# A diffusion backbone on one core: modulation sums through four 32-column groups, feed-forward loops of TensorE written out, two operands moved to 64 bytes

## The chip, the cores and the metric

The kernel runs on one core of one Trainium2 chip, in fp32. The metric is the device time of one execution in microseconds (us). TensorE (PE) multiplies, VectorE (DVE), ScalarE (ACT) and GpSimd (POOL) do elementwise work, SyncE (SP) and POOL issue transfers. PEld are TensorE's weight loads.

## The reference, cut to what matters

Two layers work on 256 latent and 256 context tokens of 1024 channels. Each has a feed-forward (2816 hidden), a mixer and a second feed-forward, and every one of them is scaled and shifted by modulation vectors, which come from one vector-matrix product with a weight of 1024 x 9216 per layer.

```python
def _swiglu(x, w_gu, w_down):
    g, u = jnp.split(x @ w_gu, 2, axis=-1)
    return (jax.nn.silu(g) * u) @ w_down
...
    silu_c = jax.nn.silu(c)
    silu_cc = jax.nn.silu(c_ctx)[None]
    h, hc = x, ctx
    for l in range(DEPTH):
...
        mod = (silu_c @ w_mod[l] + b_mod[l]).reshape(B, N_MOD, D_MODEL)
        mod_c = (silu_cc @ w_mod[l] + b_mod[l]).reshape(1, N_MOD, D_MODEL)
        m = [mod[:, i] for i in range(N_MOD)]
...
        h = h + 0.5 * m[2][:, None] * _swiglu(_modulate(_rms(h, norm_w[l, 0]), m[0], m[1]),
                                              ffn1_w_gu[l], ffn1_w_down[l])
...
        u = _modulate(_rms(h, norm_w[l, 1]), m[3], m[4])
        y, yc = _hybrid_mixer(u, uc, ctx_out, w_in[l], w_out[l], ...)
        h = h + m[5][:, None] * y
        h = h + 0.5 * m[8][:, None] * _swiglu(_modulate(_rms(h, norm_w[l, 2]), m[6], m[7]),
                                              ffn2_w_gu[l], ffn2_w_down[l])
```

## The kernel before, in words

Channels lie on partitions, the 512 tokens (latent and context) on the free axis. All weights of the feed-forwards and the mixer come as one stream of 320 blocks of 128x1024 (512 KB), loaded by SP into four places of `raw`. Every matmul is done as three, for precision: ACT rounds a block into `whi`, DVE subtracts to get `wlo` (L603), both with two places, and TensorE multiplies hi by hi, hi by lo and lo by hi (`three`, L997 to L999). A block is 24 matmuls.

A feed-forward has 44 gate and up blocks (moving operand `xh`, `xl`) and 22 down blocks (moving operand `ah`, `al`, the hidden values split in two), the latter in two halves of 11 with four banks of `ps` each. Three feed-forwards (f = 0, 1, 2) work on 512 columns, the last on 256. TensorE, ACT and DVE run the gate and up blocks in loops of four blocks, the down blocks in loops of four with the rest written out.

The modulation is cut into 36 units of 512 output columns. Units 0 to 3 are done at the start on TensorE itself (`mod_start`: a stationary operand of 2 columns, L1033, four units in four groups of 32 output partitions). For the other 32 units, POOL loads four pairs of weight rows a unit (`wm`, two places), DVE multiplies and accumulates them into `macc` (a part of `shared_a`; `mod_pair`, L621 and L625), which leaves 128 partial sums for each column and stream. `mod_sums` (L1049) then adds these over partitions: for each of four column chunks and two streams a matmul with the 128x128 products as stationary operand and a column of ones as the moving one, into a bank of `ps`; `mod_columns` on DVE (L635) adds the bias into `modc`. The sum of a unit is issued in the middle of the second block of the next round of four, and DVE may not start the next unit before it has added those columns. Units 4 to 14 belong to f = 0, unit 15 to the first mixer, 16 to 26 to f = 1, 27 to 35 to f = 2. `gate_columns` and `norm` need complete columns.

The order on each engine is the order in the code. An fp32 matmul stands as two records in the trace, an fp32r one (all of `three`) as one. In memory, `ah` and `al` start 32 bytes past a multiple of 64, since `qws` in front of them has 8 bytes and is padded to 32; `xh`, `xl`, `whi`, `wlo` start at multiples of 64.

## Time and profile before

| what | us |
|---|---|
| median of 3 runs (lowest, highest) | 1797.49 (1795.21, 1800.09) |
| span of the profiled execution | 1794.2 |
| PE busy | 1725.9 (96%) |
| PE weight loads busy | 1448.0 (81%) |
| DVE busy | 1087.9 (61%) |
| ACT busy | 613.4 (34%) |

The profiled execution has no separate time of its own; its span is 3.3 us below the median of the runs, the part that lies outside the first and last instruction. PE's busy time includes the depth of the array, so neighbouring matmuls overlap in it: what a matmul costs is read from start to start.

### The profile page before, as it was taken

Reading aid. Unit: us, or ns where it says so; the run is one execution under the profiler, and the core shown is the slowest. Engines: PE = TensorE matmul, PEld = TensorE weight load, DVE = VectorE, ACT = ScalarE, POOL = GpSimd, SP = SyncE. Lnnn points to the kernel's source line nnn. Section 1 sums busy time; section 2 is a strip of 40 time slices with the busy share of each in tenths; the row PEclk is TensorE's granted clock in tenths of the full one; section 3 lists DMA queues with packets and bytes.
Section 4 is the critical chain, followed back from the end, with each engine's and each line's share of the span. In section 5 each row is a group of like instructions: output and inputs, shape, how many; then the busy total and the mean of one; then the engine's idle time right before and its main releaser. Section 6 shows DMA issues by size and latency. Waiting matters only on the chain.

```text
span 1794.2 us, 25623 instructions
## 1 busy us (share of the span) xinstructions
PE 1725.9 (96%) x8952; PEld 1448.0 (81%) x8952; DVE 1087.9 (61%) x1668; ACT 613.4 (34%) x909; POOL 79.3 (4%) x144
## 2 busy tenths in 40 slices
PE   3999999999998999999999999999999999889999
PEld 1888888887786778888888878888888878589999
DVE  2877777235678667777761377777523277665554
ACT  3322222124534543222221242222222264554443
POOL 0000000000001000000000000000000000000000
PEclk9999999999999999999999999999999999999999
DMA  9455555322241125555552225555332224135554
GB/s 360 136 180 177 181 180 177 96 91 71 94 129 47 36 71 176 182 172 183 174 165 94 94 83 187 177 180 181 107 97 96 86 83 142 35 123 182 185 178 153
DMA packets 69685, 248.64 MB, mean 139 GB/s; under 512 B 7424, under 2 KB 8448, under 8 KB 69504
## 3 DMA queue, kind: packets, MB, share of 16 engines
q1 hardware_dynamic: 51200, 180.79, 30.9%
q0 software_dynamic: 18432, 67.12, 11.5%
q8 instruction: 36, 0.59, 0.1%
q14 instruction: 17, 0.14, 0.0%
HBM read 246.83 MB, written 1.05 MB: 138 GB/s over the span
## 4 chain that ended last, share of the span: by engine, by line
PE 89%; DVE 6%; ACT 2%; issue 1%; SPq 1%; DMA 1%; DVEq 0%; ACTq 0%
PE ps L997 28%; PE ps L999 28%; PE ps L998 27%; PE ps L1049 3%; DVE shared_b L704 1%; DVE xl L690 1%; PE ps L1188 1%; DMA raw<-wstream 1%; DVE wlo L603 1%; DVE nmax L895 1%; PE ps L1215 1%; ACT prob L505 1%; SPq L274 1%; ACT whi L343 0%; PE ps L1136 0%
## 5 line engine op out<-in xcount | busy, mean ns | idle before, releaser
L603 DVE TENSOR_TENSOR wlo<-raw,whi 128x1024 fp32r<-128x1024 f32 x320 | 392.2, 1226 | 607.6 <-ACT whi L343 606.8
L997 PE MATMUL ps<-xh,whi 128*128 128x512 f32 (+1 forms) x1880 | 679.8, 362 | 23.6 <-DVE xl L690 19.2
L343 ACT ACTIVATE whi<-raw 128x1024 fp32r<-128x1024 f32 x320 | 339.1, 1060 | 1061.9 <-PE ps L999 1045.2
L999 PE MATMUL ps<-xh,wlo 128*128 128x512 f32 (+1 forms) x1880 | 663.2, 353 | 0.0
L998 PE MATMUL ps<-xl,whi 128*128 128x512 f32 (+1 forms) x1880 | 662.5, 352 | 0.0
L997 PEld LDWEIGHTS ps<-xh,whi 128*128 128x128 f32 x1880 | 358.9, 191 | 82.3 <-issue 25.3
L998 PEld LDWEIGHTS ps<-xl,whi 128*128 128x128 f32 x1880 | 360.3, 192 | 49.3 <-issue 3.8
L999 PEld LDWEIGHTS ps<-xh,wlo 128*128 128x128 f32 x1880 | 359.8, 191 | 47.2
L625 DVE SCALAR_TENSOR_TENSOR shared_a<-wm,cs,shared_a 128x512 f32<-128x512 f32 x448 | 307.5, 746 | 0.0
L997 PE MATMUL ps<-ah,whi 128*128 (+2 forms) x704 | 258.6, 367 | 0.3 <-DVE wlo L603 0.3
L998 PE MATMUL ps<-al,whi 128*128 (+2 forms) x704 | 258.3, 367 | 0.0
L999 PE MATMUL ps<-ah,wlo 128*128 (+2 forms) x704 | 258.2, 367 | 0.0
L997 PEld LDWEIGHTS ps<-ah,whi 128*128 128x128 f32 x704 | 132.3, 188 | 24.5 <-issue 0.5
L999 PEld LDWEIGHTS ps<-ah,wlo 128*128 128x128 f32 x704 | 132.4, 188 | 24.1
L998 PEld LDWEIGHTS ps<-al,whi 128*128 128x128 f32 x704 | 132.4, 188 | 23.8
L304 POOL DMA_DIRECT2D wm<-wmod x126 | 66.6, 528 | 1143.7 <-DVEq L628 1136.0
L1049 PEld LDWEIGHTS ps<-K,shared_a 128*128 128x128 f32 x512 | 62.1, 192 | 2.7
L1049 PE MATMUL ps<-K,shared_a 128*128 128x1 f32 x512 | 58.9, 245 | 0.0
L649 DVE TENSOR_TENSOR al<-shared_b,ah 128x512 f32 (+3 forms) x88 | 54.4, 618 | 1.8 <-ACT ah L363 1.2
L642 DVE TENSOR_TENSOR shared_b<-shared_b,ps 128x512 f32<-128x512 f32 (+1 forms) x88 | 54.1, 614 | 0.6 <-ACT shared_b L358 0.5
L363 ACT ACTIVATE ah<-shared_b 128x512 f32 (+3 forms) x88 | 49.4, 561 | 5.6 <-DVE shared_b L642 5.6
L440 ACT ACTIVATE xh<-shared_b,modc 128x256 fp32r<-128x256 f32 x88 | 43.5, 508 | 22.6 <-DVE shared_b L704 22.6
(106 smaller groups left out, 872.7 us busy)
## 6 DMA issues: line engine op xcount, KB each, us to landing
raw<-wstream SPq DMA_DIRECT2D x320, 512.0 KB, 3.4
wm<-wmod POOLq DMA_DIRECT2D x128, 512.0 KB, 3.6
wm<-wmod SPq DMA_DIRECT2D x3, 2048.0 KB, 21.1
h<-x_t SPq DMA_DIRECT2D x1, 2048.0 KB, 12.0
wm<-wmod SPq DMA_DIRECT2D x2, 1024.0 KB, 20.4
K<-cols SPq DMA_DIRECT2D x1, 1163.0 KB, 14.3
out_t<-h SPq DMA_DIRECT2D x8, 128.0 KB, 2.5
K<-cols SPq DMA_DIRECT2D x1, 269.0 KB, 2.9
```

The source lines that it names most:

```text
L304: pool.dma_start(wm[:, c, :, :].rearrange("p a n -> p (a n)"), wmod[bass.ds(i * 2 + c, 1)].rearrange("a p n -> p (a n)"))\
L343: act.activation(whi[:, n % SPL, :, :].rearrange("p a b -> p (a b)"), raw[:, s, :], ACT.Copy)\
L363: act.activation(ah[:, bass.ds(i * (2 * T) + j * T, w)], af[:, j % 2, 0:w], ACT.Copy)\
L440: act.activation(xh[:, d, s * S:(s + 1) * S], xt[:, (g - 1) % 4, :], ACT.Identity, bias=modc[:, N_MOD * l + 3 * st, d, s:s + 1]).then_inc( ...
L603: dve.tensor_tensor(wlo[:, n % SPL, :, :].rearrange("p a b -> p (a b)"), raw[:, n % RAW, :], whi[:, n % SPL, :, :].rearrange("p a b -> p ( ...
L625: ins = dve.scalar_tensor_tensor(acc, src, sc, acc, ALU.mult, ALU.add)
L642: dve.tensor_tensor(af[:, j % 2, 0:w], sil[:, j % 2, 0:w], ps[:, 2 * (j % 2) + 1, 0:w], ALU.mult)\
L649: dve.tensor_tensor(al[:, dst], af[:, j % 2, 0:w], ah[:, dst].bitcast(F32), ALU.subtract)\
L997: pe.matmul(out_ap, hi_w, hi_x, start=start, stop=False)
L998: pe.matmul(out_ap, hi_w, lo_x, start=False, stop=False)
L999: return pe.matmul(out_ap, lo_w, hi_x, start=False, stop=stop)
L1049: ins = pe.matmul(ps[:, bank, 2 * c + v:2 * c + v + 1], macc[:, v, c * P:(c + 1) * P], col("one", 0, 1), start=True, stop=True)
```

## The change

`mod_sums` takes a selector as the stationary operand: 32 columns of `pick`, all zero but one, which stands at row r = 2 x unit (counted within the feed-forward) + stream. The products are the moving operand, 128 columns at a time, one chunk for each of four groups of 32 output partitions. Row r of each group gets the sums of that unit and stream; the others get zero added. So the sums of all units of a feed-forward gather in one bank. Once per feed-forward, DVE copies the bank into `mrows` (`mod_rows_out`), TensorE turns it (`mod_turn`), and DVE adds all biases at once (`mod_columns`), all in the first down half. There the banks of the two halves are chosen anew (`DN_BANKS`). Unit 15 moves from the first mixer into the first down half of f = 0, and the sum of the last unit of a full set from the end of that half to its second block. DVE waits for the sum of the unit before instead of adding its columns. TensorE's loops over blocks are written out, so are DVE's down loops. `qws` gets 64 bytes and `mrows` 512, so `shared_a`, `shared_b`, `ah`, `al` and what shares their place now start at multiples of 64 bytes.

```diff
-MIX_UNIT = 15
+LATE_UNIT = 15
+SET_ENDS = {0: 16, 1: 27, 2: 36}
-                  ("ident", P), ("poolw", DEPTH * 2 * P)):
+                  ("ident", P), ("poolw", DEPTH * 2 * P), ("pick", 64)):
...
-        qws = sb("qws", [P, DEPTH])
+        qws = sb("qws", [P, 16])
+        mrows = sb("mrows", [P, P])
...
@@ -611,6 +617,9 @@
             def mod_pair(u, p, i=0):
 
                 base = unit_steps(u)
+                if p == 0:
+
...
 
-            def mod_columns(u, n=1, i=0, bank=5):
-
-                dve.wait_ge(mod_sum, i + (u + n))
-                a = COLS["b_mod"][0] + u * UC
-                flat = modc[:, :, :, :].rearrange("p a b c -> p (a b c)")
-                dve.tensor_tensor(flat[:, bass.ds(i * UC + u * UC, n * UC)], ps[:, bank, 0:n * UC],
-                                  K[:, bass.ds(i * UC + a, n * UC)], ALU.add).then_inc(mod_col, n)
+            def mod_rows_out(f):
+
+                dve.wait_ge(mod_sum, SET_ENDS[f])
+                dve.tensor_copy(mrows[:, :], ps[:, ROWS_BANK, 0:P]).then_inc(mod_rows, 1)
+
+            def mod_columns(f):
+
+                u0, n = UNIT_AT[f][0], SET_ENDS[f] - UNIT_AT[f][0]
+                dve.wait_ge(mod_turned, f + 1)
+                turned = ps[:, TURN_BANK, 0:P].rearrange("p (j u v) -> p u j v", j=HN // P, v=2)[:, 0:n, :, :]
+                bias = col("b_mod", u0 * UC, n * UC).rearrange("p (u j v) -> p u j v", u=n, v=2)
+                flat = modc[:, :, :, :].rearrange("p a b c -> p (a b c)")[:, u0 * UC:(u0 + n) * UC]
+                dve.tensor_tensor(flat.rearrange("p (u j v) -> p u j v", u=n, v=2), turned, bias, ALU.add)\
+                    .then_inc(mod_col, n)
 
             def hidden(f, j, i, w):
...
@@ -724,23 +740,17 @@
                         elif e or not first:
 
                             hidden_low(f, e // 2 - 1, i, w)
-                        if e == 0 and columns:
-                            mod_columns(u0 - 1, 1, i)
                         if unit:
                             mod_pair(u0, e, i)
 
-                body(0, nu > 0, False, True)
+                body(0, nu > 0, True)
                 if nu:
                     with dve.Fori(1, nu) as i:
-                        body(i, True, True)
-                if 0 < nu < GU // 4:
-                    with dve.Fori(nu, nu + 1) as i:
-                        body(i, False, True)
-                if nu + 1 < GU // 4:
-                    with dve.Fori(nu + 1, GU // 4) as i:
-                        body(i, False, False)
+                        body(i, True)
+                if nu < GU // 4:
+                    with dve.Fori(max(nu, 1), GU // 4) as i:
+                        body(i, False)
                 hidden_low(f, -1, GU // 4, w)
-                gate_columns(m)
 
                 def half_out(hf, ds):
                     for d in ds:
...
@@ -756,12 +766,16 @@
 
                 for hf in range(2):
                     nd = n0 + GU + HALF * hf
-                    split_next(nd)
-                    with dve.Fori(0, (HALF - 3) // 4) as i:
-                        for e in range(4):
-                            split_next(nd + 1 + e, i, 1)
-                    if hf == 0 and nu == GU // 4:
-                        mod_columns(u0 + nu - 1, bank=0)
+                    for b in range(HALF - 2):
+                        split_next(nd + b)
+                        if hf == 0 and f == 0 and 1 <= b <= PAIRS:
+                            mod_pair(LATE_UNIT, b - 1)
+                        if hf == 0 and nu and b == HALF - 4:
+                            mod_rows_out(f)
+                    if hf == 0:
+                        if nu:
+                            mod_columns(f)
+                        gate_columns(m)
 
                     for b in (HALF - 2, HALF - 1):
                         if hf == 0:
...
@@ -860,10 +874,6 @@
                         lambda_ends()
                     if 1 <= b <= QKB:
                         rope(l, b - 1)
-                    if l == 0 and QKB < b <= QKB + PAIRS:
-                        mod_pair(MIX_UNIT, b - QKB - 1)
-                    if l == 0 and b == QKB + PAIRS + 2:
-                        mod_columns(MIX_UNIT)
                     if b in (CV - 3, CV - 2):
 
                         dve.wait_ge(evac, EV[l] + b)
...
-            def mod_sums(u, i=0, bank=5):
-
-                pe.wait_ge(mod_acc, i * (2 * DC) + unit_steps(u + 1))
-
-                pe.wait_ge(mod_col, i + u)
-                for c in range(HN // P):
-                    for v in range(2):
-                        ins = pe.matmul(ps[:, bank, 2 * c + v:2 * c + v + 1], macc[:, v, c * P:(c + 1) * P],
-                                        col("one", 0, 1), start=True, stop=True)
+            def mod_sums(f, u):
+
+                pe.wait_ge(mod_acc, unit_steps(u + 1))
+                for v in range(2):
+                    r = 2 * (u - UNIT_AT[f][0]) + v
+                    for j in range(HN // P):
+                        ins = pe.matmul(ps[32 * j:32 * j + 32, ROWS_BANK, 0:P], col("pick", 31 - r, 32),
+                                        macc[:, v, j * P:(j + 1) * P], start=r == 0,
+                                        stop=u + 1 == SET_ENDS[f] and v == 1)
                 ins.then_inc(mod_sum, 1)
+
+            def mod_turn(f):
+
+                pe.wait_ge(mod_rows, f + 1)
+                pe.transpose(ps[:, TURN_BANK, 0:P], mrows[:, :], col("ident", 0, P)).then_inc(mod_turned, 1)
 
             def norm_stat(m):
...
-                    for e in range(2 if first else 0, 4):
-                        if e % 2 == 0 and not first:
-
-                            pe.wait_ge(mul_done, i * 2 + (F0 + e // 2 - 1))
-
-                        column_block(n0 + e, e, w, i, 1,
-                                     between=(lambda: mod_sums(u0 - 1, i)) if e == 1 and sums else None)
-
-                body(0, False, True)
+                first_blocks(m, n0)
+                for i in range(GU // 4):
+                    for e in range(2 if i == 0 else 0, 4):
+                        if e % 2 == 0 and i:
+
+                            pe.wait_ge(mul_done, F0 + 2 * i + e // 2 - 1)
+                        sums = e == 1 and 1 <= i <= nu
+                        column_block(n0 + 4 * i + e, e, w,
+                                     between=(lambda u=u0 + i - 1: mod_sums(f, u)) if sums else None)
+
+                def down(hf, b):
+                    n = n0 + GU + HALF * hf + b
+                    pe.wait_ge(lo_done, n + 1)
+                    if hf == 0:
+
+                        pe.wait_ge(al_done, F0 + 2 * b + 2)
+
+                    last = b == HALF - 1 and hf == 1
+                    for r, d in [(r, d) for d in range(4) for r in range(2)] if last else \
+                            [(r, d) for r in range(2) for d in range(4)]:
+                        if hf == 0 and b == 0 and d == 3:
+
+                            pe.wait_ge(mul_done, F0 + FC - 1)
+                        src = slice((2 * b + r) * T, (2 * b + r) * T + w)
+                        ins = three(ps[:, DN_BANKS[hf][d], 0:w], whi[:, n % SPL, 4 * r + d, :],
+                                    wlo[:, n % SPL, 4 * r + d, :], ah[:, src], al[:, src],
+                                    b == 0 and r == 0, b == HALF - 1 and r == 1)
+                        if last and r == 1 and d < 3:
+                            ins.then_inc(dn_done, 1)
+                    ins.then_inc(block_done, 1)
+
+                for b in range(HALF):
+                    down(0, b)
+                    if nu == GU // 4 and b == 1:
+                        mod_sums(f, u0 + nu - 1)
+                    if f == 0 and b == 6:
+                        mod_sums(f, LATE_UNIT)
+                    if nu and b == 8:
+                        mod_turn(f)
                 if nu:
-                    with pe.Fori(1, min(nu + 1, GU // 4)) as i:
-                        body(i, True)
-                if nu + 1 < GU // 4:
-                    with pe.Fori(nu + 1, GU // 4) as i:
-                        body(i, False)
-                for hf in range(2):
-                    nd = n0 + GU + HALF * hf
-                    b0 = 4 if hf == 0 else 0
-
-                    def down(b, i=0, k=0):
-                        n = nd + b
-                        pe.wait_ge(lo_done, i * (4 * k) + (n + 1))
-                        if hf == 0:
-
-                            pe.wait_ge(al_done, i * (8 * k) + (F0 + 2 * b + 2))
-
-                        last = b == HALF - 1 and hf == 1
-                        for r, d in [(r, d) for d in range(4) for r in range(2)] if last else \
-                                [(r, d) for r in range(2) for d in range(4)]:
-                            src = bass.ds(i * (8 * T * k) + (2 * b + r) * T, w)
-                            ins = three(ps[:, b0 + d, 0:w], whi[:, n % SPL, 4 * r + d, :],
-                                        wlo[:, n % SPL, 4 * r + d, :], ah[:, src], al[:, src],
-                                        b == 0 and r == 0, b == HALF - 1 and r == 1)
-                            if last and r == 1 and d < 3:
-                                ins.then_inc(dn_done, 1)
-                        ins.then_inc(block_done, 1)
-
-                    if nu:
-
-                        pe.wait_ge(mod_col, u0 + (min(nu, GU // 4 - 1) if hf == 0 else nu))
-                    down(0)
-                    with pe.Fori(0, (HALF - 3) // 4) as i:
-                        for e in range(4):
-                            down(1 + e, i, 1)
-                    if hf == 0 and nu == GU // 4:
-
-                        mod_sums(u0 + nu - 1, bank=0)
-                    down(HALF - 2)
-                    down(HALF - 1)
+
+                    pe.wait_ge(mod_col, SET_ENDS[f])
+                    pe.wait_ge(mod_rows, f + 1)
+                for b in range(HALF):
+                    down(1, b)
...
@@ -1148,12 +1156,8 @@
                         column_block(n0 + b, b % 4, T if b < 4 else w)
                     if 1 <= b <= QKB:
                         stat(b - 1)
-                    if l == 0 and b == QKB + PAIRS + 1:
-                        mod_sums(MIX_UNIT)
 
                 pe.wait_ge(rq_done, 8 * (l + 1))
-                if l == 0:
-                    pe.wait_ge(mod_col, MIX_UNIT + 1)
                 for b in range(VB):
                     n = n0 + CV + b
                     pe.wait_ge(lo_done, n + 1)
```

TensorE, gate and up of f = 0, second block of a round, where a unit's sum stands between two chunks (`K` holds the constants, `shared_a` the products). Before:

```order
L998 MATMUL ps<-xl,whi 128x512
L999 MATMUL ps<-xh,wlo 128x512
L1044 REGISTER_ALU
L1046 REGISTER_ALU
L1049 MATMUL ps<-K,shared_a 128x1 x8
L997 MATMUL ps<-xh,whi 128x512
L998 MATMUL ps<-xl,whi 128x512
```

After:

```order
L1008 MATMUL ps<-xl,whi 128x512
L1009 MATMUL ps<-xh,wlo 128x512
L1058 MATMUL ps<-shared_a,K 32x128 x8
L1007 MATMUL ps<-xh,whi 128x512
L1008 MATMUL ps<-xl,whi 128x512
```

The eight matmuls stay where they were; their output is 32x128 instead of 128x1, and the register arithmetic of the loop is gone.

DVE, f = 0, from the end of the gate and up loop to the end of the first down half (`wlo` is the split of a weight block, `mrows` the copied bank). Before:

```order
L649 TENSOR_TENSOR al<-shared_b,ah 128x512
L655 TENSOR_SCALAR gcol<-modc 128x16
L603 TENSOR_TENSOR wlo<-raw,whi 128x1024
L760 UNCONDITIONAL_BRANCH
...
L603 TENSOR_TENSOR wlo<-raw,whi 128x1024
L760 REGISTER_ALU
L760 COMPARE_AND_BRANCH
L635 TENSOR_TENSOR modc<-ps,K 128x8
L603 TENSOR_TENSOR wlo<-raw,whi 128x1024 x2
L661 SCALAR_TENSOR_TENSOR h<-ps,gcol,h 128x256 x4
```

After:

```order
L609 TENSOR_TENSOR wlo<-raw,whi 128x1024 x2
L630 TENSOR_SCALAR shared_a<-wm,cs 128x512 x2
L634 SCALAR_TENSOR_TENSOR shared_a<-wm,cs,shared_a 128x512 x2
L609 TENSOR_TENSOR wlo<-raw,whi 128x1024
L634 SCALAR_TENSOR_TENSOR shared_a<-wm,cs,shared_a 128x512 x4
...
L609 TENSOR_TENSOR wlo<-raw,whi 128x1024 x3
L642 COPY mrows<-ps 128x128
L609 TENSOR_TENSOR wlo<-raw,whi 128x1024
L651 TENSOR_TENSOR modc<-ps,K 128x96
L671 TENSOR_SCALAR gcol<-modc 128x16
L609 TENSOR_TENSOR wlo<-raw,whi 128x1024 x2
```

The passes of unit 15 stand between the splits, and the copy, the add of all columns and the gate columns near the end of the half.

## Rows read from the trace of the kernel before

**Rows 1.** The page: busy time and share, granted clock, chain by line.
```profile
PE 1725.9 (96%) x8952; PEld 1448.0 (81%) x8952; DVE 1087.9 (61%) x1668; ACT 613.4 (34%) x909; POOL 79.3 (4%) x144
PEclk9999999999999999999999999999999999999999
PE ps L997 28%; PE ps L999 28%; PE ps L998 27%; PE ps L1049 3%; DVE shared_b L704 1%; DVE xl L690 1%; PE ps L1188 1%; DMA raw<-wstream 1%; DVE wlo L603 1%; DVE nmax L895 1%; PE ps L1215 1%; ACT prob L505 1%; SPq L274 1%; ACT whi L343 0%; PE ps L1136 0%
```

**Rows 2.** Chain that ended last, in time: start, length, engine, output, line, records.
```profile
75.15 1.68 PE ps L1049 x16
98.75 1.68 PE ps L1049 x16
```

**Rows 3.** Timeline of PE around one sum: start, length, engine, line, operation, output<-inputs, form.
```profile
74.75 0.40 PE L999 MATMUL ps<-xh,wlo 128*128 128x512 f32 x1
74.98 1.84 PE L1049 MATMUL ps<-K,shared_a 128*128 128x1 f32 x16
76.69 0.48 PE L997 MATMUL ps<-xh,whi 128*128 128x512 f32 x1
...
79.54 0.39 PE L997 MATMUL ps<-xh,whi 128*128 128x512 f32 x1
...
98.35 0.40 PE L999 MATMUL ps<-xh,wlo 128*128 128x512 f32 x1
```

**Rows 4.** Timeline of PE at the start, units 0 to 3 (three windows).
```profile
22.80 0.59 PE L1060 MATMUL ps<-shared_a,K 128*128 128x512 f32 x1
...
23.33 0.61 PE L1033 MATMUL ps<-wm,cs 128*2 128x512 f32 x4
...
23.33 3.62 PE L1033 MATMUL ps<-wm,cs 128*2 128x512 f32 x32
```

**Rows 5.** Groups by line and form: count, busy us, mean ns, idle before.
```profile
L625 DVE SCALAR_TENSOR_TENSOR shared_a<-wm,cs,shared_a 128x512 f32<-128x512 f32 x448 | 307.5, 746 | 0.0
...
L1215 PE MATMUL ps<-difT,vt 128*128 128x128 f32 x160 | 23.0, 283 | 8.7 <-ACT difT L515 8.7
...
L1033 PE MATMUL ps<-wm,cs 128*2 128x512 f32 x64 | 7.6, 592 | 4.3 <-DMA wm<-wmod 4.3
```

**Rows 6.** Timeline of PE in the mixer's attention.
```profile
579.54 1.16 PE L1215 MATMUL ps<-difT,vt 128*128 128x128 f32 x8 [0.88 <-ACT difT L515]
```

**Rows 7.** Timeline of PE: down, value blocks, gate and up, down with 256 columns.
```profile
304.18 0.40 PE L997 MATMUL ps<-ah,whi 128*128 128x512 f32 x1
...
354.34 0.40 PE L999 MATMUL ps<-ah,wlo 128*128 x1
...
539.68 0.39 PE L997 MATMUL ps<-whi,xh 128*128 128x512 f32 x1
...
545.58 0.39 PE L999 MATMUL ps<-whi,xl 128*128 128x512 f32 x1
...
1639.78 0.28 PE L998 MATMUL ps<-xl,whi 128*128 128x256 f32 x1
...
1643.26 0.28 PE L997 MATMUL ps<-xh,whi 128*128 128x256 f32 x1
...
1786.69 0.28 PE L999 MATMUL ps<-ah,wlo 128*128 128x256 f32 x1
...
1791.31 0.28 PE L999 MATMUL ps<-ah,wlo 128*128 128x256 f32 x1
```

**Rows 8.** Timeline of DVE: gate and up, then down; in brackets idle time and releaser.
```profile
100.69 0.17 DVE L635 TENSOR_TENSOR modc<-ps,K 128x8 f32 x1 [0.35 <-PE ps L1049]
...
111.23 1.23 DVE L603 TENSOR_TENSOR wlo<-raw,whi 128x1024 fp32r<-128x1024 f32 x1 [0.96 <-ACT whi L343]
...
322.27 1.23 DVE L603 TENSOR_TENSOR wlo<-raw,whi 128x1024 fp32r<-128x1024 f32 x1 [4.37 <-ACT whi L343]
```

**Rows 9.** Timeline of PE where the first mixer's scores begin.
```profile
558.49 1.02 PE L1188 MATMUL ps<-kq 128*128 128x512 f32 x2
```

More of the change, by code:

```diff
@@ L66 @@
 UNIT_AT = {0: (4, GU // 4), 1: (16, GU // 4), 2: (27, 9)}
-MIX_UNIT = 15
+LATE_UNIT = 15
+SET_ENDS = {0: 16, 1: 27, 2: 36}
+ROWS_BANK, TURN_BANK = 5, 1
+DN_BANKS = ((4, 6, 7, 0), (1, 2, 3, 5))
 COLS = {}
@@ L72 @@
 for _name, _n in (("c", DC * 2), ("norm_w", DEPTH * 3 * DC * 2), ("b_mod", DEPTH * N_MOD * DC * 2),
-                  ("eps", 1), ("one", 1), ("sel", 8), ("ones", P),
+                  ("eps", 1), ("sel", 8), ("ones", P),
                   ("qw", DEPTH), ("kw", DEPTH), ("subln", DEPTH), ("conv", DEPTH * 2 * 3),
@@ L176, in program @@
         mod_sum = sem("mod_sum")
+        mod_rows = sem("mod_rows")
+        mod_turned = sem("mod_turned")
         mod_col = sem("mod_col")
@@ L613, in mod_pair @@
                 base = unit_steps(u)
+                if p == 0:
+                    dve.wait_ge(mod_sum, i + u)
                 dve.wait_ge(wm_in[p % 2], i * (16 * PAIRS // 2) + 16 * (((u - START_UNITS) * PAIRS + p) // 2 + 1))
@@ L717, in ffn, with body @@
                 u0, nu = UNIT_AT.get(f, (0, 0))
-                def body(i, unit, columns, first=False):
+                def body(i, unit, first=False):
                     for e in range(4):
@@ L840, in lambda_sums @@
                 dve.sem_inc(lam_red, 1)
-                own(dve.tensor_scalar(qws[:, :], col("qw", 0, DEPTH), DH ** -0.5, None, ALU.mult))
+                own(dve.tensor_scalar(qws[:, 0:DEPTH], col("qw", 0, DEPTH), DH ** -0.5, None, ALU.mult))
             def lambda_ends():
@@ L999, in three, with column_block @@
                 return pe.matmul(out_ap, lo_w, hi_x, start=False, stop=stop)
-            def column_block(n, bank, w, i=0, k=0, ready=None, a=0, last=True, between=None):
-                pe.wait_ge(lo_done, i * (4 * k) + (n + 1))
+            def column_block(n, bank, w, ready=None, a=0, last=True, between=None):
+                pe.wait_ge(lo_done, n + 1)
                 for c in range(DC):
@@ L1069, in ffn @@
                 F0 = FC * f
-                def body(i, sums, first=False):
-                    if first:
-                        first_blocks(m, n0)
-                    for e in range(2 if first else 0, 4):
-                        if e % 2 == 0 and not first:
-                            pe.wait_ge(mul_done, i * 2 + (F0 + e // 2 - 1))
-                        column_block(n0 + e, e, w, i, 1,
-                                     between=(lambda: mod_sums(u0 - 1, i)) if e == 1 and sums else None)
@@ L1347 @@
         "eps": np.full((P, 1), EPS),
-        "one": np.ones((P, 1)),
+        "pick": np.repeat((np.arange(64) == 31)[None], P, 0),
         "sel": np.stack([np.arange(P) == 32 * u + v for u in range(4) for v in range(2)], 1),
```

6 lines of the change are left out of this document (3 added, 3 removed).

## The prediction

> **What bounds the kernel now.** I read the page from the top: PE is busy 96% of the span and DVE 61%, and the clock digits are 9 in all forty slices, so the array is at its upper level (2.4 GHz) nearly throughout [rows 1]. The chain that ended last runs through PE for almost all of its length, and one small line in it has 3%: L1049, the modulation sums. The bound is therefore the pitch of TensorE (start of one matmul to start of the next) and the number of matmuls, not a wait. Next I read the chain in order of time: the 32 sums stand in it one by one (two are shown), each 16 records in 1.68 us [rows 2], that is 0.105 us a record although only one column is moved: with one moving column the time is that of loading 128 columns of products as the stationary operand. 32 x 1.68 = 53.8 us, the 3%.
>
> **What one sum really costs.** In the timeline of TensorE around one sum [rows 3] the last matmul before it starts at 74.75, the sum at 74.98, the next matmul at 76.69. From 79.54 to 98.35 there are 83 pitches, 18.81/83 = 0.2266 us, and the back edge of the written loop lies among them: it costs nothing. From 76.69 to 79.54 there are 12 pitches in 2.85 us where 2.72 were due: 0.13 us are lost after the sum. So a sum costs 1.71 + 0.13 = 1.84 us, and the chain's period agrees: 98.75 - 75.15 = 23.60 [rows 2], and 96 x 0.2266 + 1.84 = 23.59. Of 32 sums that is 58.9 us, 3.3% of the span; this is the pot that the first edit draws on.
>
> **Part 1, sums by four column groups.** Removed are, for each unit, 8 matmuls with the products stationary (16 records, since fp32 runs as two). Added are 8 matmuls with a 128x32 selector stationary and 128 columns of products moving, again 16 records, written to four different groups of 32 partitions. What four groups do side by side is in this trace: the start of the program has the same scheme with 2-column stationaries. Four records stand there within 0.61 us although each takes 0.592, and 32 records took 3.62 us, so (3.62 - 0.61)/7 = 0.43 us a burst of four [rows 4, 5]. A burst of four costs what one record of 512 columns costs. Scaled to 128 columns that is 0.107 us; the nearest row with 128 moving columns in fp32 is L1215, 8 records in 1.16 us of which the last is 0.28 long, so (1.16 - 0.28)/7 = 0.126 us [rows 5, 6]. I take 0.126, because its stationary loads are of real size: four bursts are 0.50 us.
> Going into the groups: the last 128-wide record before the start's grouped ones began at 22.80, the first grouped one at 23.33 [rows 4]; 0.53 where 0.43 was due, so 0.10 us. Coming out: no row shows it. Its low bound is zero, its high one the whole length of a 128-column record less its pitch, 0.28 - 0.11 = 0.17; I take 0.17 because the other direction wasn't free. The 0.13 after the sum stays. Sum: 0.10 + 0.50 + 0.17 + 0.13 = 0.90 us instead of 1.84, a gain of 0.94, and 32 x 0.94 = 30.1 us. Low bound for a sum: 4 x 0.107 = 0.43 with nothing around it, a gain of 45 us. High bound with groups that still overlap: 1.3 us (another 0.11 for the first loads of 32 columns, and bursts of 0.2), a gain of 17 us.
> The row shows 0.10 us on the way into the groups. The Trainium skill (TensorEngine Tiling (Array Packing), Key Properties) says that changing the tiling mode, and not merely the tile, drains the engine; the trace agrees in kind. The rule speaks against this edit, because it is paid twice in each of 32 places; by a full drain both ways (0.17 each instead of 0.10 and 0.17) the sum would be 0.97 us and the gain 28 us.
>
> **Part 2, ah and al moved from 32 to 64 bytes.** `qws` grows from 2 to 16 columns, and everything allocated behind it, from `shared_a` on, starts at a multiple of 64 bytes; before it was 32 past one. The down matmuls (moving ah, al) have a pitch of (354.34 - 304.18)/215 = 0.2333 us, those of gate and up (moving xh, xl, which lie on 64 already) 0.2266 [rows 3, 7]. The difference is 6.7 ns, 16 cycles at 2.4 GHz. It isn't the change of bank after every third matmul: the value blocks of the mixer change it just so and run at (545.58 - 539.68)/26 = 0.2269 [rows 7]. It isn't the loop either, since it begins with the first block, which is written out. Three feed-forwards of 512 columns have 22 x 24 = 528 such matmuls each: 1584 x 6.7 ns = 10.6 us. The last feed-forward has 256 columns, and there the picture is turned round: ah at (1791.31 - 1786.69)/39 = 0.1185, xh at (1643.26 - 1639.78)/29 = 0.1200 [rows 7]. So alignment gives nothing there and could cost 528 x 1.5 ns = 0.8 us; I take zero, with that as bound. Since the 256-column rows don't show the effect, the 10.6 us are the less certain part.
>
> **Part 3, loops of TensorE written out.** Nothing: the back edges cost nothing above, and the straight-line value blocks run at the same pitch as the looped ones.
>
> **Part 4, the turn.** Each of three feed-forwards gets a copy of 128x128 and one add of 96 columns on DVE, and one 128-column transpose on TensorE: 0.126 + 0.13 behind it, about 0.25 us, 0.8 us for three. In exchange 32 small adds on DVE go. The copy is queued behind the split of block 7 of the down part, some 3 us before TensorE reaches the end of block 8, where the turn stands; DVE idles 4.37 us of every 5.6 there (24 x 0.2333) [rows 8]. TensorE's new wait for the columns stands ahead of the second half, two blocks later. Both are covered; uncovered, each would cost the DVE chain of about 1 us, 3 us in all. The selector adds 63 columns to a load of constants, most of them in its second, late part, and the bank numbers change no instruction; both nothing.
>
> **Part 5, unit 15 from mixer to down part.** Its four pairs (16 DVE passes of 0.746 us, 2.98 a block [rows 5]) go into the idle 4.37 us of blocks 1 to 4, its four loads with them. They leave the mixer, where TensorE starts the first scores at 558.49 with no idle time noted ahead of them [rows 9], so nothing is won there beyond the sum already counted. On DVE the first pair of every unit now waits for the sum before it, at the place where the column add waited before (0.35 us [rows 8]); the sum is shorter, so this gets less. In the gate and up loop the period falls from 23.6 to 22.7 us, all of it in the block that holds the sum; in the fullest blocks, of 5.44 us, DVE still waits 0.96 us for ACT, which waits for TensorE [rows 8]: DVE does not take over. If it did, the bound is the 0.96 us of that block against the 0.94 that the period falls, so nothing comes on top of the forecast's range.
>
> **The sum.** 1794.2 - 30.1 - 10.6 + 0.8 = 1754.3 us of span. The median of the runs, 1797.49, lies 3.3 above the profiled span, so I expect **1757.6 us**, 2.2% less.
>
> **Rivals.**
> (a) The groups overlap, but alignment isn't the cause of the 6.7 ns. For it speaks that the 256-column rows go the other way, and that after a sum even the aligned xh runs at (79.54 - 76.69)/12 = 0.2375 for a while [rows 3]. Time: 1768.
> (b) The groups work in bursts that don't overlap with each other: each of four bursts takes a record's full length and its loads, 0.28 + 0.11, so 1.56 + 0.40 = 1.96 us a sum, no gain; only alignment is left: 1797.5 - 10.6 + 0.8 + 3.8 = 1791. Against it: the bursts at the start follow at 0.43 with records of 0.59.
> (c) The other side, **slower**: the 32-column loads and the moving columns take turns in the array, so that 16 records go one by one, at 0.105 for the load and 0.107 for the columns: 3.4 us + 0.4 = 3.8 us a sum, 32 x 1.96 = 63 us more, less 9.8: 1850. It decides the sign from 2.15 us a sum on (1.84 + 9.8/32). For it: no row has a 32-column stationary in this mode, and both records of one product go to the same group. Against it: the start has the same two records to a group, and overlaps four.
> (d) A sum near its low bound, 0.5 to 0.6 us: 1797.5 - 41 - 10 = 1746.
>
> **How the numbers follow.** Forecast (sum of 0.7 to 1.2 us, alignment works) 0.62; (a) 0.16; (d) 0.10; (b) 0.07; (c) 0.04; 0.01 for another loss. The forecast's own bounds are 1751 (0.7 us) and 1767 (1.2 us). The range has to reach into (a) and (d): 1747 to 1771 leaves out about 2 in 10. This kernel's measurement can tell about 0.3% from no change: (b) lies on that border and is split. Faster by over 0.3%: 0.92; within: 0.04; slower: 0.04.
>
> **What would show it.** In the profile of the changed kernel: the 16 records of a sum at 0.4 to 0.6 us from first to last start; 22.66 us from one sum to the next instead of 23.60; pitch of the down matmuls 0.2267 instead of 0.2333, and 0.1185 to 0.1200 in the last feed-forward; no idle time of TensorE ahead of the turns and of the second down halves. It would be wrong if the sum's records start 0.1 us apart one by one, if the down pitch stays at 0.2333, or if DVE's split becomes the releaser of gate and up matmuls.

## The result, and the profile after

The changed kernel takes 1756.43 us (median; 1754.53 to 1756.91), the kernel before beside it 1798.53 us: a ratio of 0.9763, 95% interval 0.975 to 0.9776. It is 42.1 us faster; 1757.6 had been forecast. The profiled span fell from 1794.2 to 1755.1 us, by 39.1; why that is less stands under "The sum of it" below.

The page of the changed kernel: busy time, granted clock, chain by line (`three` is now L1007 to L1009, the sums L1058).

```profile
PE 1687.6 (96%) x8955; PEld 1405.1 (80%) x8955; DVE 1082.3 (62%) x1642; ACT 613.9 (35%) x909; POOL 79.3 (5%) x144
...
PEclk9999999999999999999999999999999999999999
...
PE ps L1007 29%; PE ps L1008 28%; PE ps L1009 28%; PE ps L1058 1%; DVE shared_b L720 1%; PE ps L1192 1%; DMA raw<-wstream 1%; DVE wlo L609 1%; DVE nmax L905 1%; PE ps L1219 1%; DVE xl L706 1%; SPq L280 1%; ACT prob L511 1%; PE ps L1144 0%; ACT whi L349 0%
```

TensorE is still the bound. The sums have gone from 3% of the chain [rows 1] to 1%. The chain in order of time, as [rows 2]:

```profile
74.81 0.57 PE ps L1058 x16
97.41 0.57 PE ps L1058 x16
```

Sixteen records and the way back now take 0.57 us instead of 1.68, and the period is 22.60 instead of 23.60 us. The timeline of TensorE around a sum, as [rows 3]:

```profile
74.42 0.39 PE L1009 MATMUL ps<-xh,wlo 128*128 128x512 f32 x1
74.74 0.64 PE L1058 MATMUL ps<-shared_a,K 128*32 128x128 f32 x16
75.31 0.50 PE L1007 MATMUL ps<-xh,whi 128*128 128x512 f32 x1
...
78.66 0.39 PE L1009 MATMUL ps<-xh,wlo 128*128 128x512 f32 x1
```

In: 74.74 - 74.42 - 0.2267 = 0.09 us. The sixteen records and the way out: 0.57. Behind it: 14 pitches in 3.35 us where 3.17 were due, 0.18. Together 0.84 us a sum. The last of the sixteen records starts 0.37 us behind the first (0.64 less its own length of 0.27), so they overlap.

The down part, 48 matmuls of 512 columns, then 256 columns (before in [rows 7]), and the turn between them in time:

```profile
293.75 0.39 PE L1007 MATMUL ps<-ah,whi 128*128 128x512 f32 x1
...
304.40 0.39 PE L1009 MATMUL ps<-ah,wlo 128*128 128x512 f32 x1
...
344.16 0.39 PE L1009 MATMUL ps<-ah,wlo 128*128 128x512 f32 x1
344.39 0.27 PE L1066 MATMUL ps<-K,mrows 128*128 128x128 f32 x1
344.42 0.48 PE L1007 MATMUL ps<-ah,whi 128*128 128x512 f32 x1
...
349.29 0.39 PE L1007 MATMUL ps<-ah,whi 128*128 128x512 f32 x1
...
1699.73 0.28 PE L1007 MATMUL ps<-ah,whi 128*128 128x256 f32 x1
...
1710.88 0.28 PE L1007 MATMUL ps<-ah,whi 128*128 128x256 f32 x1
```

(304.40 - 293.75)/47 = 0.2266 us, where it was 0.2333; with 256 columns (1710.88 - 1699.73)/93 = 0.1199, where it was 0.1185. The turn has no idle time ahead of it. DVE in the first down half, where it now works on unit 15 (idle time before a split in brackets, as [rows 8]):

```profile
318.78 2.73 DVE L634 SCALAR_TENSOR_TENSOR shared_a<-wm,cs,shared_a 128x512 f32<-128x512 f32 x4
323.08 1.23 DVE L609 TENSOR_TENSOR wlo<-raw,whi 128x1024 fp32r<-128x1024 f32 x1 [1.56 <-ACT whi L349]
...
341.38 0.28 DVE L642 COPY mrows<-ps 128x128 f32<-128x128 f32 x1
```

Of the idle 4.37 us of a block 1.56 are left: the passes fit, and the copy is done 2.7 us before the turn.

### The profile page after: what moved, and what is told of

The parts are those of the page before. It is cut to its first block, busy times and chain, and to the rows that moved or that the text cites. A ratio compares the mean times of both kernels' runs of the same rounds, so it can differ in the third digit from the quotient of the medians.

```text
span 1755.1 us, 24815 instructions
## 1 busy us (share of the span) xinstructions
PE 1687.6 (96%) x8955; PEld 1405.1 (80%) x8955; DVE 1082.3 (62%) x1642; ACT 613.9 (35%) x909; POOL 79.3 (5%) x144
## 4 chain that ended last, share of the span: by engine, by line
PE 90%; DVE 6%; ACT 2%; SPq 1%; issue 1%; DMA 1%; DVEq 0%; ACTq 0%
PE ps L1007 29%; PE ps L1008 28%; PE ps L1009 28%; PE ps L1058 1%; DVE shared_b L720 1%; PE ps L1192 1%; DMA raw<-wstream 1%; DVE wlo L609 1%; DVE nmax L905 1%; PE ps L1219 1%; DVE xl L706 1%; SPq L280 1%; ACT prob L511 1%; PE ps L1144 0%; ACT whi L349 0%
## 5 line engine op out<-in xcount | busy, mean ns | idle before, releaser
L1007 PE MATMUL ps<-xh,whi 128*128 128x512 f32 (+1 forms) x1880 | 682.4, 363 | 23.4 <-DVE xl L706 18.3
L1009 PE MATMUL ps<-xh,wlo 128*128 128x512 f32 (+1 forms) x1880 | 664.4, 353 | 0.0
L1007 PEld LDWEIGHTS ps<-xh,whi 128*128 128x128 f32 x1880 | 359.5, 191 | 87.6 <-issue 31.0
L1009 PEld LDWEIGHTS ps<-xh,wlo 128*128 128x128 f32 x1880 | 360.6, 192 | 47.6
L1007 PE MATMUL ps<-ah,whi 128*128 128x512 f32 (+1 forms) x704 | 255.9, 364 | 0.0
L1008 PE MATMUL ps<-al,whi 128*128 128x512 f32 (+1 forms) x704 | 255.4, 363 | 0.0
L1009 PE MATMUL ps<-ah,wlo 128*128 128x512 f32 (+1 forms) x704 | 255.3, 363 | 0.0
L1007 PEld LDWEIGHTS ps<-ah,whi 128*128 128x128 f32 x704 | 132.3, 188 | 21.3 <-issue 0.6
L1009 PEld LDWEIGHTS ps<-ah,wlo 128*128 128x128 f32 x704 | 132.3, 188 | 20.6
L677 DVE SCALAR_TENSOR_TENSOR h<-ps,gcol,h 128x256 f32<-128x256 f32 x88 | 38.2, 478 | 18.6 <-PE ps L1009 18.6
L364 ACT ACTIVATE shared_b<-ps 128x512 f32<-128x512 f32 (+1 forms) x88 | 46.5, 528 | 0.0
## 6 DMA issues: line engine op xcount, KB each, us to landing
h<-x_t SPq DMA_DIRECT2D x1, 2048.0 KB, 11.7
```

The lines of the kernel that those rows point to most:

```text
L364: act.activation(sil[:, j % 2, 0:w], ps[:, 2 * (j % 2), 0:w], ACT.Silu).then_inc(silu_done, 1)
L1007: pe.matmul(out_ap, hi_w, hi_x, start=start, stop=False)
L1008: pe.matmul(out_ap, hi_w, lo_x, start=False, stop=False)
L1009: return pe.matmul(out_ap, lo_w, hi_x, start=False, stop=stop)
```

## The experiments

Every time below is a median; each kernel has its own ratio to the kernel before, run beside it. Its medians in these runs lie between 1798.53 and 1800.22 us, so a difference of two medians from different runs is good to some 2 us; the pitches and periods of the traces are finer. A "visit" is one stay of TensorE in the four groups.

### Alignment: the edit alone, and undone

The kernel before with the wider `qws` alone:

```diff
-        qws = sb("qws", [P, DEPTH])
+        qws = sb("qws", [P, 16])
...
```

> The kernel before with one edit: qws has 16 columns, so that ah and al (and all behind qws) start on 64 bytes. Theory (alignment of the moving operand sets the pitch of the 512-column down matmuls): pitch 0.2333 becomes 0.2267 in three feed-forwards, 1584 x 6.7 ns = 10.6 us less, and 528 x 1.6 ns = 0.8 us more in the last feed-forward, where the pitch goes from 0.1184 to 0.1200; together 9.8 us less, about 1788 us. Rival (the pitch comes from the order of banks or from the place of the down part in the program): 0.2333 stays, no change.

Measured: 1790.52 us, ratio 0.994 (0.9917 to 0.9963), 9.5 us under the 1800.03 of the kernel before beside it. The down pitch is (350.93 - 309.90)/181 = 0.2267:

```profile
309.90 0.39 PE L999 MATMUL ps<-ah,wlo 128*128 128x512 f32 x1
...
350.93 0.39 PE L997 MATMUL ps<-ah,whi 128*128 x1
```

The changed kernel with ah and al alone moved back by 32 bytes:

```diff
         hidden = ExitStack()
+        hidden.enter_context(nc.sbuf_tensor("hpad", [P, 8], F32))
```

> The changed kernel with 32 bytes of padding in front of ah, so that ah and al alone start at 32 past a multiple of 64; all else as changed. Theory (it is the moving operand of the down matmuls that counts): the pitch returns to 0.2333 with 512 columns and to 0.1184 with 256, 9.8 us more than the changed kernel, about 1766 us. Rival (it is another of the operands that moved with them, for example what DVE and ACT write at the same time): the pitch stays at 0.2267 and the time at 1756 us.

Measured: 1765.29 us, ratio 0.9806 (0.9784 to 0.9828), 8.9 us over the changed kernel. 512 columns, then 256:

```profile
294.75 0.40 PE L1008 MATMUL ps<-ah,whi 128*128 128x512 f32 x1
...
300.82 0.40 PE L1010 MATMUL ps<-ah,wlo 128*128 128x512 f32 x1
...
1719.75 0.28 PE L1009 MATMUL ps<-al,whi 128*128 128x256 f32 x1
...
1730.50 0.28 PE L1008 MATMUL ps<-ah,whi 128*128 128x256 f32 x1
```

26 pitches of 0.2335, and 92 of 0.1168. So it is the place of ah and al and no other operand. With 256 columns the pitch is even shorter than before the change (0.1185), although both start "32 past 64". The addresses of the built programs tell the two apart: before, ah and al start 96 past a multiple of 128, here 32 past one.

### The same for xh and xl

```diff
+        xpad0 = sb("xpad0", [P, 8])
         xh = sb("xh", [P, DC, T], F32R)
         xl = sb("xl", [P, DC, T], F32R)
+        xpad1 = sb("xpad1", [P, 8])
```

> The changed kernel with 32 bytes of padding in front of xh and again behind xl, so that xh and xl start at 32 past a multiple of 64 and all else stays on 64. Theory: every 512-column matmul with xh or xl moving goes from 0.2267 to 0.2333: 3 x 44 x 24 = 3168 in gate and up, and about 20 x 24 = 480 in the first mixer, 3648 x 6.7 ns = 24 us more; those with 256 columns go from 0.1200 to 0.1184, 1056 + some 500, 2.5 us less; about 1778 us. Rival (a property of ah and al or of the down part): 1756 us.

Measured: 1774.8 us, ratio 0.9862 (0.9836 to 0.9888), 18.4 us over the changed kernel. Gate and up with 512 columns, down with 512, gate and up with 256, down with 256:

```profile
59.72 0.39 PE L1011 MATMUL ps<-xh,wlo 128*128 128x512 f32 x1
...
70.46 0.39 PE L1009 MATMUL ps<-xh,whi 128*128 128x512 f32 x1
...
369.67 0.39 PE L1009 MATMUL ps<-ah,whi 128*128 128x512 f32 x1
...
380.43 0.39 PE L1011 MATMUL ps<-ah,wlo 128*128 128x512 f32 x1
...
1619.78 0.28 PE L1010 MATMUL ps<-xl,whi 128*128 128x256 f32 x1
...
1630.28 0.28 PE L1010 MATMUL ps<-xl,whi 128*128 128x256 f32 x1
...
1726.94 0.28 PE L1009 MATMUL ps<-ah,whi 128*128 128x256 f32 x1
...
1739.90 0.28 PE L1011 MATMUL ps<-ah,wlo 128*128 128x256 f32 x1
```

Gate and up: 46 pitches of 0.2335, as the theory says. The two paddings together also moved ah and al by 64 bytes, to 64 past a multiple of 128, which I hadn't meant to matter; their pitch is (380.43 - 369.67)/47 = 0.2289, between 0.2267 and 0.2333. With 256 columns xh runs at 90 pitches of 0.1167, and ah at (1739.90 - 1726.94)/110 = 0.1178. So the 256-column matmuls with xh gained twice what I had put down for them, but ah and al lost 1584 x 2.2 ns = 3.5 us that the forecast didn't have, and gained 528 x 2.2 ns = 1.2 us. With the forecast's counts the pitches give 24.8 - 5.1 + 3.5 - 1.2 = 22 us, close to the forecast's 21.5, and not the 18.4 of the medians; the difference isn't explained, and the interval of this run alone is 5 us to each side.

### Loops of TensorE written out, in the kernel before

```diff
-                    with pe.Fori(1, min(nu + 1, GU // 4)) as i:
-                        body(i, True)
...
+                for i in range(1, GU // 4):
+                    body(i, 1 <= i <= nu)
...
-                    with pe.Fori(0, (HALF - 3) // 4) as i:
+                    for i in range((HALF - 3) // 4):
```

> The kernel before with TensorE's loops over blocks written out and nothing else. Theory: back edges cost nothing on a TensorE that is never waiting for its sequencer, so no change: 1797.5 us within 1. Rival (the loops cost where the trace doesn't show it, or straight-line code starves TensorE, since it must be fetched, 0.6 MB more of it): a change of 2 us or more either way.

Measured: 1797.52 us, ratio 0.999 (0.9979 to 1.0001). The interval holds 1, but it also holds a gain of 2 us or more, so the times alone don't rule out the rival. The chain does, for the back edges and for starving in gate and up: one period is 23.60 us, to the hundredth that of the looped kernel [rows 2].

```profile
74.06 1.68 PE ps L1049 x16
97.66 1.68 PE ps L1049 x16
```

DVE's written-out down loops weren't run by themselves.

### Sums: how the 0.84 us is made up

Every unit's grouped matmuls issued twice:

```diff
+                for v in range(2):
+                    r = 2 * (u - UNIT_AT[f][0]) + v
+                    for j in range(HN // P):
+                        ins = pe.matmul(ps[32 * j:32 * j + 32, spare, 0:P], col("pick", 31 - r, 32),
+                                        macc[:, v, j * P:(j + 1) * P], start=True, stop=True)
                 ins.then_inc(mod_sum, 1)
...
```

> The changed kernel with every unit's eight grouped matmuls issued a second time, straight behind the first and into another bank that nobody reads. It measures the second sixteen records without a second change of shape around them. Theory (the sum of 0.85 us is some 0.43 to 0.50 us of four bursts and the rest is going in and out of the groups and the slow pitch after it): 32 x 0.43 to 0.50 = 14 to 16 us more. Rival (bursts are all of it, nothing is fixed): 0.85 each, 27 us more.

Measured: 1768.16 us, ratio 0.9827 (0.9811 to 0.9844), 11.7 us over the changed kernel, where 14 to 16 were expected. In the chain the period is 23.00 us, 0.40 more than 22.60:

```profile
73.93 0.57 PE ps L1058 x16
96.93 0.57 PE ps L1058 x16
```

Sixteen further records cost 0.40 us of the period, so of a sum's 0.84 the other 0.44 are paid once a visit. The timeline gives the parts:

```profile
73.86 0.64 PE L1058 MATMUL ps<-shared_a,K 128*32 128x128 f32 x16
...
74.88 0.50 PE L1007 MATMUL ps<-xh,whi 128*128 128x512 f32 x1
...
78.18 0.39 PE L1009 MATMUL ps<-xh,wlo 128*128 128x512 f32 x1
```

From the first record to the next 128-wide start it is 1.02 us, 0.57 in the changed kernel: sixteen records take 0.44 to 0.45, 0.11 a burst of four, and the way out is 0.57 - 0.44 = 0.13. Behind the visit 14 pitches take 3.30 us, 0.13 too many and not 0.18; that is the step from 0.44 to the 0.40 of the period, and why the slow stretch is shorter here stays open. The records cost what was expected of them (0.43 to 0.50); that the stretch behind them gets shorter was not foreseen.

The sums of all units but the first of each set left out:

```diff
                 pe.wait_ge(mod_acc, unit_steps(u + 1))
+                if u > UNIT_AT[f][0]:
+                    pe.sem_inc(mod_sum, 1)
+                    return
...
```

> The changed kernel with the grouped matmuls of the first unit of each set alone; those of the other 29 units are left out (their modulation is missing from the output), the signals stay. Theory: 29 x 0.85 = 24.7 us less than the changed kernel, about 1732 us, if TensorE stays the bound to the end. Rival (DVE's accumulation of the next unit or the weight splits become the bound once the sum is gone): a smaller gain, with idle time of TensorE ahead of gate and up blocks.

Measured: 1731.05 us, ratio 0.9617 (0.9601 to 0.9633), 25.4 us less than the changed kernel (24.7 expected), 0.88 us a sum. The waits of TensorE for the split (microseconds in total, times, longest) stay as small as in the changed kernel, where they are 3.0 us:

```profile
PE ps L1007 <- DVE wlo L609: 3.7, 4, 1.5
```

So neither DVE nor ACT takes over when the sums are gone.

### Is it the groups or the smaller stationary operand

All eight matmuls sent to one group:

```diff
-                        ins = pe.matmul(ps[32 * j:32 * j + 32, ROWS_BANK, 0:P], col("pick", 31 - r, 32),
+                        ins = pe.matmul(ps[0:32, ROWS_BANK, 0:P], col("pick", 31 - r, 32),
...
```

> The changed kernel with the eight 32-column matmuls of a unit all sent to the same group of 32 output partitions (the four chunks are added together, so the modulation is wrong). Theory (the gain comes from four groups at once): the sixteen records follow each other at 0.107 to 0.126 us, a sum costs 1.7 to 2.0 us plus some 0.4 around it, 2.1 to 2.4 us, 40 to 50 us more than the changed kernel, as slow as before or slower. Rival (the gain comes from small stationary loads, not from groups at once): 1756 to 1765 us.

Measured: 1796.13 us, ratio 0.9981 (0.9972 to 0.9991), 39.7 us over the changed kernel.

Selectors of 128 columns, across the whole array:

```diff
-                        ins = pe.matmul(ps[32 * j:32 * j + 32, ROWS_BANK, 0:P], col("pick", 31 - r, 32),
+                        ins = pe.matmul(ps[:, ROWS_BANK, 0:P], col("pick", 127 - 32 * j - r, P),
...
```

> The changed kernel with selectors of 128 columns instead of 32: the same eight matmuls with products moving and the same result in the bank, but across the whole array, with no change of shape and nothing side by side. Theory: sixteen records at 0.126 us and 0.13 behind, 2.15 us a sum, 32 x 1.3 = 42 us more than the changed kernel, about 1798 us. Rival (loads of 128 columns hide behind the moving columns): 0.107 a record, 1.85 us, 32 us more.

Measured: 1788.53 us, ratio 0.9937 (0.9921 to 0.9954), 32.1 us over the changed kernel. The chains, first of one group, then of the wide selector:

```profile
74.53 1.86 PE ps L1058 x16
98.38 1.86 PE ps L1058 x16
```

```profile
75.10 1.78 PE ps L1058 x16
98.68 1.78 PE ps L1058 x16
```

The way into the wide selector's records:

```profile
74.70 0.40 PE L1009 MATMUL ps<-xh,wlo 128*128 128x512 f32 x1
74.94 1.95 PE L1058 MATMUL ps<-shared_a,K 128*128 128x128 f32 x16
```

Periods of 23.85 and 23.58 us against 21.76 without a sum (96 x 0.2267): 2.09 and 1.82 us a sum. The rival of the second run was right: loads of 128 columns hide behind 128 moving columns, at some 0.11 us a record (1.78/16), so turning the operands round gains nothing and costs nothing by itself (1.82 against 1.84). The whole gain of the first edit is the four groups at once; with one group the fixed part of the visit makes it dearer than before. The wide selector, which changes no shape of the stationary operand, pays 0.01 us on the way in (74.94 - 74.70 - 0.2267), where four groups and one pay 0.09: so that part goes with the change to 32 columns. The wide kernel lies 11.2 us under the 1799.74 of the kernel before beside it; alignment explains 9.8 of them by the pitches, 32 x 0.02 us the sums, and the rest is within the spread.

### The last feed-forward started 32 bytes further on, and the changed kernel once more

```diff
+OFF = (0, 0, 0, 8)
+XOFF = (0, 0, 0, 0, 0, 8)
...
-                        src = slice((2 * b + r) * T, (2 * b + r) * T + w)
+                        src = slice((2 * b + r) * T + OFF[f], (2 * b + r) * T + OFF[f] + w)
...
-                            xh[:, c, a:w], xl[:, c, a:w], c == 0, c == DC - 1)
+                            xh[:, c, a + off:w + off], xl[:, c, a + off:w + off], c == 0, c == DC - 1)
```

> The changed kernel, and in the last feed-forward (256 columns) xh, xl, ah and al are written and read 8 columns (32 bytes) further on in their places, so that the moving operands of 1056 gate and up and 528 down matmuls start 32 past a multiple of 64. All else as changed. Theory (with 256 columns the 32-byte start is the quicker one, as ah before the change): pitch 0.1200 becomes 0.1184 in both, 1584 x 1.6 ns = 2.5 us less than the changed kernel, about 1754 us. Rival (0.1184 belongs to the down part alone): only 0.8 us less, and gate and up stay at 0.1200.

Measured: 1753.16 us, ratio 0.9735 (0.9721 to 0.9748). Gate and up run at (1622.90 - 1620.43)/21 = 0.1176, down at (1710.39 - 1699.78)/91 = 0.1166.

```profile
1620.43 0.28 PE L1011 MATMUL ps<-xh,wlo 128*128 128x256 f32 x1
...
1622.90 0.28 PE L1011 MATMUL ps<-xh,wlo 128*128 128x256 f32 x1
...
1699.78 0.28 PE L1010 MATMUL ps<-al,whi 128*128 128x256 f32 x1
...
1710.39 0.28 PE L1011 MATMUL ps<-ah,wlo 128*128 128x256 f32 x1
```

> The changed kernel once more, as it is, on the chip of the run before it. It gives the time to compare that run with, and a second profile: the three stretches at half clock that were 6.8 us long in the first profile where the kernel before had 3.4 may be shorter again (theory: how long TensorE stays at the lower clock after a pause varies from run to run, worth 1 to 3 us of span) or the same (rival: the changed order of work fixes them).

Measured: 1755.85 us, ratio 0.9758 (0.9745 to 0.9772). The run before it is 2.7 us faster than this one; the intervals of the two touch, so it is the pitches that show the effect, and the time only agrees. By the pitches the gain should be 1056 x 2.4 ns + 528 x 3.3 ns = 4.3 us; the same edit on top of the pairs below gave 4.6.

The clock of two stretches of 9 us, each with a restart of TensorE after a norm: the first feed-forward of the second layer, and the last feed-forward (columns as given by the profile: stretch, length, busy time of PE, PEld, DVE, ACT, POOL, granted clock, DMA share, GB/s). The kernel before, the changed kernel, and the changed kernel once more:

```profile
659.00:668.00 9.00, 6.75 (x35) 5.91 (x36) 8.96 (x24) 6.44 (x14) 0.00 (x0) 0.81 0.17 61
1598.00:1607.00 9.00, 7.73 (x46) 7.18 (x47) 7.11 (x16) 4.89 (x9) 0.00 (x0) 0.81 0.19 60
```

```profile
645.00:654.00 9.00, 7.90 (x34) 7.12 (x34) 9.00 (x24) 5.93 (x13) 0.00 (x0) 0.62 0.19 58
1557.00:1566.00 9.00, 7.09 (x32) 6.79 (x33) 6.48 (x17) 4.69 (x9) 0.00 (x0) 0.62 0.19 58
```

```profile
645.00:654.00 9.00, 8.53 (x49) 7.63 (x50) 9.00 (x24) 5.62 (x12) 0.00 (x0) 0.81 0.08 33
1557.00:1566.00 9.00, 7.82 (x36) 7.34 (x37) 6.26 (x16) 4.68 (x9) 0.00 (x0) 0.62 0.18 60
```

TensorE pauses there for the norm and restarts at its lower level (1.2 GHz). A granted clock of 0.81 over 9 us is 3.4 us at the lower level, 0.62 is 6.8 us. The restart at 645 was long in one execution of the changed kernel and short in the other, so its length isn't a property of the change. The second profile is no shorter on the whole, though: its mean clock is 0.988 like the first one's.

### Two units in one visit

A second place for the products (unit u uses place u mod 2), so that DVE can go on while two units wait to be summed:

```diff
-        macc = shared_a[:, 0:2 * HN].rearrange("p (v n) -> p v n", v=2)
+        macc_d = sb("macc_d", [P, HN])
+        MACC = ((shared_a[:, 0:HN], shared_a[:, HN:2 * HN]), (shared_a[:, 2 * HN:3 * HN], macc_d[:, :]))
...
-                        sums = e == 1 and 1 <= i <= nu
+                        done = [u0 + i - 2, u0 + i - 1] if i % 2 == 0 and 2 <= i <= nu else \
+                            [u0 + i - 1] if nu < GU // 4 and i == nu and nu % 2 else []
+                        sums = e == 1 and done
...
```

> The changed kernel with a second place for the accumulated products (unit u uses place u mod 2), so that two units are summed in one go: 17 visits to the four groups instead of 32, and the same 32 x 16 records. DVE's gate and up loops that accumulate are written out for it. Theory (a sum of 0.85 us is 0.40 of records, which the run with every sum twice measured, and 0.45 fixed: going in and out and the slow pitch after it): 15 x 0.45 = 6.7 us less than the changed kernel, about 1749 us. Rival (the fixed part is paid per record or grows with the number of records): no change, 1756 us.

Measured: 1749.51 us, ratio 0.9723 (0.971 to 0.9736), 6.9 us less than the changed kernel. The chain:

```profile
96.84 1.01 PE ps L1059 x32
141.59 1.01 PE ps L1059 x32
```

Two rounds with one visit take 44.75 us; 192 x 0.2267 = 43.53, so a visit with two units costs 1.22 us, and 0.84 + 0.40 = 1.24 was expected. The fixed part is paid once a visit, as the theory says.

> The kernel of the run before and, in the last feed-forward, moving operands that start 32 bytes further on (the run with that edit alone was 2.7 us under the changed kernel). Theory: the two add up, 6.7 + 2.7 = 9.4 us less than the changed kernel, about 1747 us, the fastest of all. Rival: another wait takes a part back, more than 1750 us.

Measured: 1744.94 us, ratio 0.9699 (0.9686 to 0.9712). This is the fastest kernel: 11.5 us under the changed kernel, some 2 us more than the 9.4 expected, which is within the spread of the runs.

## Why the prediction was right, point by point

**Sums.** Forecast 0.90 us a sum, 30.1 us in all; measured 0.84 us, 32 x 1.00 = 32 us. The parts: in, 0.10 forecast and 0.09 measured; four bursts, 0.50 and 0.44; out, 0.17 and 0.13; behind it, 0.13 and 0.18. I had scaled the burst by 512/128 to 0.107 and then gone to 0.126, the row with 128-column loads; the scaled value was the nearer one. The size of the loads wasn't what makes that row slow, since the wide selector's records with 128-column loads go at 0.11 too; what does stays open. In and out are paid in each visit, as the runs with two sums in a row show (0.44 fixed). That the way in costs what the start of the program showed, and the way out no less, agrees with the Trainium skill's rule (TensorEngine Tiling (Array Packing), Key Properties) that a change of the tiling mode drains the engine; no run here separates a drain from any other cause of the 0.22 us of in and out.

**Rivals of the sums.** (b) fell, since bursts follow at 0.11 us and not at 0.39, and (c), since sixteen records take 0.57 us with the way out and not 3.4. The run with one group, where all sixteen go one by one, shows what (c)'s mechanism costs: 2.09 us, not 3.8, since loads hide behind the moving columns even within one group. That is just under the 2.15 at which the sign would turn, and the kernel is still 0.2% faster than before: (c) was priced far too high, and even with it the change would have been about even.

**Alignment.** Forecast 10.6 us for 1584 matmuls, pitch 0.2333 to 0.2267; measured just that pitch, by the edit alone (9.5 us less in all, with 0.8 the other way in the last feed-forward) and by its undoing (8.9 us more). Rival (a) fell. The last feed-forward was the open point: I took zero and gave 0.8 us as the bound; the loss is 528 x 1.5 ns = 0.8 us, the bound. "At a multiple of 64" was the wrong condition, and right here by luck: the padding happened to bring ah and al from 96 past a multiple of 128 to 0, and at 64 a third of the gain would have been missing.

**Loops written out.** Forecast nothing; the period is the same 23.60 us, and the ratio 0.999 has an interval that holds 1.

**Turn, unit 15, new waits.** The turn costs TensorE some 0.14 us a time (from 344.16, 22 matmuls and the turn take 5.13 us, where 22 x 0.2267 = 4.99 were due), not 0.25. Nobody waits for it, nor DVE for the sums: the wait of 0.35 us [rows 8] is gone from the list of DVE's waits.

**The sum of it.** 32.0 + 10.5 - 0.8 - 0.4 = 41.3 us; the medians differ by 42.1, the profiled spans by 39.1. Where the spans' 2.2 us are: in the profile before, all three restarts named here spend 3.4 us at the lower level, in the profile after 6.8. The first 120 matmuls from such a restart took 20.42, 20.02 and 16.63 us before (from 435.20 to 455.62, 660.88 to 680.90, 1599.27 to 1615.90), and 21.22, 21.20 and 17.69 after (from 421.37 to 442.59, 645.83 to 667.03, 1558.91 to 1576.60), 3.0 us more in all; 0.8 us the other way aren't assigned.

The profile before was a quick execution: 44 others of the kernel before have spans of 1793.6 to 1800.7 us, each 1.6 or 1.7 below the time of its run. So the 3.3 us between its span and the median were not just what lies outside the first and last instruction, as I had written: half of them were this. The nearness of the forecast is in part luck. For the span (1754.3, measured 1755.1) the dearer estimate of the sum and a longer time at the lower clock nearly cancelled. For the median (1757.6, measured 1756.43) the gain came out 2.2 us larger than forecast, 42.1 instead of 39.9, and the median of the kernel before 1.0 us higher.

## What to carry to other kernels

Where a small reduction over partitions interrupts a stream of large matmuls, send it through four groups of 32 output partitions and gather as many of them as memory allows in one visit: a visit costs 0.44 us here, with one sum in it or with two, and each sixteen records 0.40. Look at the pitch of the same matmul in different parts of a kernel: a difference of 3% with the same shape was the start address of the moving operand. Try the moves at 32, 64 and 96 past a multiple of 128 bytes, for each number of columns: the best was another one for 256 columns than for 512. A term read from rows of the same program (the start's grouped matmuls) was good to 0.1 us, though no row had the exact shape.

## What the runs showed of the hardware that was not expected

The pitch of an fp32r matmul depends on where its moving operand starts relative to a multiple of 128 bytes, and the best place depends on the number of columns. Addresses are those of the built programs:

| start past a multiple of 128 | 512 columns | 256 columns |
|---|---|---|
| 0 | 0.2267 | 0.1200 |
| 32 | 0.2335 | 0.1167 |
| 64 | 0.2289 | 0.1178 |
| 96 | 0.2333 | 0.1185 |

So "on 64 bytes" isn't the condition for 0.2267: in the run with xh and xl moved, ah and al started on a multiple of 64 and lost a third of the gain. With 512 columns the rows for 32 and 96 are the same within what such stretches can tell. Each row but the first rests on one or two placings, and the row for 64 on a by-product of a run meant for something else. The high and the low part (xh and xl, ah and al) were always moved together, so no run tells whether both must be in place. Why 256 columns prefer 32 stays open, as does that gate and up of the last feed-forward ran at 0.1167 with the whole of xh moved and at 0.1176 with the columns shifted within it, at the same start address.
